# The last expert item of a mixture-of-experts loop handled apart: other items' rows added early, its own output by halves through a one-hot product

## What is computed

```python
def moe_swiglu(h, router, w1, w3, w2):
    logits = (xt @ router).astype(jnp.float32)
    top_val, top_idx = lax.top_k(logits, TOP_K)          # 2 of 8
    gates = jax.nn.softmax(top_val, axis=-1)
    combine = jnp.sum(jax.nn.one_hot(top_idx, N_EXPERTS) * gates[..., None], axis=1)
    out = jnp.zeros((B * T, D), jnp.float32)
    for e in range(N_EXPERTS):
        out = out + combine[:, e:e + 1] * swiglu(xt, w1[e], w3[e], w2[e])
    return out
...
h = h + moe_swiglu(u, m_router[c], m_w1[c], m_w3[c], m_w2[c])
return rmsnorm(h, norm_final)
```

## Time and profile before

| | us |
|---|---|
| median of 3 runs | 1728.95 (1728.02 to 1730.25) |
| the profiled execution's own time | 1729.75 |
| its span | 1727.9 |
| PE busy in the span | 1619.8 (94%) |
| DVE busy | 1234.2 (71%) |
| ACT busy | 966.2 (56%) |
| POOL busy | 43.6 (3%) |

### The profile page before, as it was taken

How to read it: one execution, slowest core, us unless ns; L and a number is a source line. 1 busy time by engine, 2 the same in 40 slices (tenths; PEclk the granted TensorE clock), 3 DMA queues, 4 the chain that set the end, 5 groups by cost and what they waited for, 6 DMA issues and landing times.

```text
span 1727.9 us, 25936 instructions
## 1 busy us (share of the span) xinstructions
PE 1619.8 (94%) x10286; PEld 1360.6 (79%) x10286; DVE 1234.2 (71%) x928; ACT 966.2 (56%) x780; POOL 43.6 (3%) x25
## 2 busy tenths in 40 slices
PE   4999889899979997889999999999999999999993
PEld 3777875899869886778888888888888888888883
DVE  4575345555447444489888898898898898988985
ACT  2321222444333344367777777777777777777773
POOL 1000500000000000010000000000000000000000
PEclk9999999999989998989999999999999999999997
DMA  4447213555544452379999999999999999999972
GB/s 165 146 146 264 81 52 126 192 176 191 193 163 170 164 193 70 133 300 421 375 369 406 357 389 388 358 404 387 346 412 364 374 391 366 395 387 352 411 305 85
DMA packets 70893, 473.76 MB, mean 274 GB/s; under 512 B 7728, under 2 KB 7856, under 8 KB 17840
## 3 DMA queue, kind: packets, MB, share of 16 engines
q1 hardware_dynamic: 66512, 456.69, 69.0%
q10 hardware_dynamic: 3168, 11.96, 1.8%
q0 software_dynamic: 1152, 4.19, 0.7%
HBM read 452.37 MB, written 20.45 MB: 274 GB/s over the span
## 4 chain that ended last, share of the span: by engine, by line
issue 56%; PE 37%; DVE 4%; ACT 1%; DMA 1%; POOL 0%; DVEq 0%; POOLq 0%; ACTq 0%
PE ps L1218 36%; DVE mem L965 0%; PE ps L1230 0%; ACT workr L577 0%; DVE mem L859 0%; DMA work<-back,itab 0%; DMA h<-x 0%; ACT work L561 0%; DVE work L1051 0%; PE ps L1566 0%; DVE work L815 0%; POOL sent L537 0%; DVE mem L951 0%; DVE h L843 0%; DVE pairs_r L835 0%
## 5 line engine op out<-in xcount | busy, mean ns | idle before, releaser
L1218 PE MATMUL ps<-pairs_r,workr 128*128 128x512 f32 x2856 | 659.5, 389 | 1.8 <-DVE workr L1057 1.8
L1218 PEld LDWEIGHTS ps<-pairs_r,workr 128*128 128x128 f32 x2856 | 535.3, 188 | 112.7 <-DVE workr L1057 2.0
L1218 PE MATMUL ps<-workr 128*128 128x512 f32 x2016 | 481.2, 392 | 2.5 <-DVE workr L1156 2.5
L1218 PEld LDWEIGHTS ps<-workr 128*128 128x128 f32 x2016 | 374.2, 188 | 78.9 <-issue 2.7
L1168 DVE TENSOR_TENSOR workr<-ring,workr 128x2048 fp32r<-128x2048 f32 x168 | 383.3, 2290 | 58.3 <-ACT workr L746 58.3
L1168 DVE TENSOR_TENSOR pairs_r<-ring,pairs_r 128x2048 fp32r<-128x2048 f32 x168 | 382.0, 2290 | 22.5 <-ACT pairs_r L746 20.0
L746 ACT ACTIVATE pairs_r<-ring 128x2048 fp32r<-128x2048 f32 x168 | 322.6, 1920 | 112.6 <-PE ps L1218 110.4
L746 ACT ACTIVATE workr<-ring 128x2048 fp32r<-128x2048 f32 x168 | 321.2, 1917 | 43.8 <-PE ps L1218 39.2
L1218 PE MATMUL ps<-mem 64*64 64x64 f32 (+8 forms) x3384 | 251.3, 267 | 28.5 <-DVE mem L859 11.1
L1218 PEld LDWEIGHTS ps<-mem 64*64 64x64 f32 (+5 forms) x3384 | 193.8, 154 | 84.9 <-issue 60.0
L835 DVE TENSOR_TENSOR pairs_r<-ring,pairs_r 128x2048 fp32r<-128x2048 f32 x68 | 156.0, 2294 | 145.7 <-ACT pairs_r L585 144.5
(11 more groups left out here) (195 smaller groups left out, 574.9 us busy)
## 6 DMA issues: line engine op xcount, KB each, us to landing
ring<-mstream SPq DMA_DIRECT2D x336, 1024.0 KB, 6.9
ring<-pstream SPq DMA_DIRECT2D x65, 1024.0 KB, 4.9
mem<-rstream SPq DMA_DIRECT2D x10, 2048.0 KB, 8.2
sent<-work SPq DMA_DIRECT2D x1, 6144.0 KB, 19.3
back<-work SPq DMA_DIRECT2D x1, 6144.0 KB, 35.5
back<-work ACTq DMA_DIRECT2D x9, 512.0 KB, 8.8
work<-sent ACTq DMA_DIRECT2D x8, 512.0 KB, 7.8
h<-x SPq DMA_DIRECT2D x1, 1024.0 KB, 6.3
```

What stands on the lines that cost most here:

```text
L1218: ins = nc.tensor.matmul(*args, **kw)
```

## The change

- The loops of PE, ACT and DVE run one item less; the last item is written out behind them by the same function with `last` set. In it ACT no longer fetches tokens for a next item, the four dummy units and the gather are gone, and SP's dummy fetches with them.
- POOL gathers rows from `back` during the last item, as soon as the output of the item before it has landed there. What the last item owes is still zero in `back`. DVE adds the four tiles at steps j = 2 to 5 of the last item.
- Which rows of the last item belong to which token is put into two one-hot matrices `hot` on DVE ahead of the loop; PE transposes them at the start of the last item, and DVE stores them as `hotT`.
- The last w2 product (`output_by_halves`) finishes bank 4 and then bank 5. Each half is split in a high and a low part (ACT, DVE), and PE multiplies `hotT` by them, which puts the last item's output rows at their tokens: eight matmuls in all. DVE adds the four results times the gate (`share`, L1265 of the new file) to `h`.
- The final norm sums squares of four half tiles, multiplies tile 0 by the gain before the root is there, and writes the output in two DMAs.

The core of the diff (helpers, new semaphores and buffer addresses left out):

```diff
 # SP
-            for n in range(AHEAD):
-                i = PRE + NE * E_UNITS + n
-                sp.wait_ge(s_lo, extras * E_UNITS + (i - RING + 1))
-                sp.dma_start(unit(i)[:, 0:64], mstream[n, :, 0:64]).then_inc(s_w[i % RING], 16)
-            sp.wait_ge(s_fin, TT)
-            sp.dma_start(out, xn_).then_inc(s_out, 16)
+            for t in range(TT):
+                sp.wait_ge(s_fin, t + 1)
+                sp.dma_start(out[:, t, :], xn_[:, t, :]).then_inc(s_out, 16)
 # POOL
-            pool.wait_ge(s_yall, 1)
-            for t in range(TT):
-                for n in range(2):
-                    nc.gpsimd.indirect_dma_start(
-                        yg[:, t, n, :], None, back, bass.IndirectOffsetOnAxis(itab[:, 8 + 2 * t + n:9 + 2 * t + n], 0)
-                    ).then_inc(s_yl[2 * t + n], 16)
+            pool.wait_ge(s_sent, 64)
+            pool.wait_ge(s_yw, extras * 16 + 16 * (NE + 1))
+            pool.wait_ge(s_hotp, 1)
+            link(nc.gpsimd.tensor_tensor(rw(332, 4), rw(50, 4), ones[:, 0:4], ALU.mult))
+            for i in range(2 * TT):
+                nc.gpsimd.indirect_dma_start(
+                    fetched[i], None, back, bass.IndirectOffsetOnAxis(itab[:, 8 + i:9 + i], 0)
+                ).then_inc(s_yl[i], 16)
 # ACT, behind the loop
-            store_output(extras + NE)
-            a.wait_ge(s_yw, extras * 16 + 16 * (NE + 2))
-            act_f(small[:, 190:191], ones[:, 0:1], ACT.Sqrt).then_inc(s_yall, 1)
+            with a.Fori(0, extras + (NE - 1)) as e:
+                item(e, False)
+            item(extras + (NE - 1), True)
+            a.preload_act_table(ACT.Sqrt)
+            for c in range(2):
+                a.wait_ge(s_lo6, c + 1)
+                act_f(yh[:, c * 512:(c + 1) * 512], ps[:, 4 + c, :], ACT.Copy).then_inc(s_yh, 1)
+            for i, (c, t, _) in enumerate(spread):
+                a.wait_ge(s_hf, 2 * TT + i + 1)
...
+                act_f(junk[:, 0:512], hv[:, t, c * 512:(c + 1) * 512], ACT.Square, scale=1.0 / 32.0,
+                      accum_out=ss[:, 8 + 2 * c + t:9 + 2 * c + t]).then_inc(s_ss, 1)
 # DVE, ahead of the loop: loc, inl, share and the one-hot matrices, 11 instructions; in the last item
+                    if last and j == 0:
+                        v.wait_ge(s_hotp, 1)
+                        V.tensor_copy(hotT, ps[:, 2, 0:256]).then_inc(s_hotT, 1)
...
+                    if last and 2 <= j < 2 + 2 * TT:
+                        add_fetched(j - 2)
 # DVE, behind it
+            for c in range(2):
+                cs = slice(c * 512, (c + 1) * 512)
+                v.wait_ge(s_yh, c + 1)
+                V.tensor_tensor(yl[:, cs], ps[:, 4 + c, :], yh[:, cs].bitcast(F32), ALU.subtract).then_inc(s_ylo, 1)
+            for i, (c, t, bank) in enumerate(spread):
+                v.wait_ge(s_last, i + 1)
+                dst = hv[:, t, c * 512:(c + 1) * 512]
+                V.scalar_tensor_tensor(out=dst, in0=ps[:, bank, :], scalar=rw(328 + t, 1), in1=dst, op0=ALU.mult,
+                                       op1=ALU.add).then_inc(s_hf, 1)
...
+            V.tensor_tensor(hg, hv[:, 0, :], gfin, ALU.mult).then_inc(s_hg, 1)
+            V.scalar_tensor_tensor(out=m, in0=ss[:, 8:10], scalar=EPS, in1=ss[:, 10:12], op0=ALU.add,
+                                   op1=ALU.add).then_inc(s_ms, 1)
+            rsqrt(m, r, small[:, 184:186])
+            V.tensor_scalar(xn_[:, 0, :], hg, r[:, 0:1], None, ALU.mult).then_inc(s_fin, 1)
+            V.scalar_tensor_tensor(out=xn_[:, 1, :], in0=hv[:, 1, :], scalar=r[:, 1:2], in1=gfin, op0=ALU.mult,
+                                   op1=ALU.mult).then_inc(s_fin, 1)
 # PE: output_by_halves
+                    for c in range(2):
+                        for half in range(2):
+                            for g in range(2):
+                                ins = M3(ps[:, 4 + c, :], parts((actTh, actTl), i % 2, 2 * half + g),
+                                         parts(w[half], g, slice(c * 512, (c + 1) * 512)),
+                                         start=False, stop=(half == 1 and g == 1), skip_group_check=True)
+                        ins.then_inc(s_lo6, 1)
 # PE, behind the last item
+            for c in range(2):
+                mine = [x for x in spread if x[0] == c]
+                cs = slice(c * 512, (c + 1) * 512)
+                if c:
+                    pe.wait_ge(s_ylo, 1)
+                pe.wait_ge(s_yh, c + 1)
+                for _, t, bank in mine:
+                    M(ps[:, bank, :], hotT[:, t * P:(t + 1) * P], yh[:, cs], start=True, stop=False)
+                pe.wait_ge(s_ylo, c + 1)
+                for _, t, bank in mine:
+                    M(ps[:, bank, :], hotT[:, t * P:(t + 1) * P], yl[:, cs], start=False, stop=True).then_inc(s_last, 1)
```

More of the change, by code:

```diff
@@ L419, in first_unit @@
             return 6 * j - 2 if j else 0
+        spread = [(0, 0, 0), (0, 1, 1), (1, 0, 2), (1, 1, 3)]
         block = ctx.enter_context(nc.Block())
@@ L738, in _, with item @@
             a.preload_act_table(ACT.Silu)
-            with a.Fori(0, extras + NE) as e:
+            def item(e, last):
                 def split_e(lo, hi):
@@ L759, in _ @@
                     split_e(u, u + 1)
-                    if j == 2:
+                    if j == 2 and not last:
                         a.wait_ge(s_sent, 64)
@@ L1621, in _, with item @@
             extras = pe.value_load(itab[0:1, 0:1], min_val=0, max_val=EXTRA)
-            with pe.Fori(0, extras + NE) as e:
+            def item(e, last):
                 def units(n, dims, **sizes):
```

119 lines of the change are left out of this document (84 added, 35 removed).

## The result

The changed kernel took 1709.42 us, the median of 5 runs (1708.97 to 1718.04), against 1728.95 before (5 runs, 1724.91 to 1730.25). The ratio is 0.9897, with a 95% interval of 0.988 to 0.9914. The profiled execution took 1709.88 with a span of 1708.1.

The account below looks back on a forecast made before the run. PE was taken to bound the items, with a chain without PE behind them. Tail -14.8 and end of the last product -0.6 make -15.4; from the median 1728.95 that gives 1713.5 us, range 1712.0 to 1717.5.

Parts of the forecast that it names:

- The bound and the cover: Items: PE sets the time, so work beside it on DVE, ACT or DMAs is free until their reserve is used.
- E: End of the last w2 product, forecast to move by -0.6 us: gather's transposes save 0.8, one-hot transposes cost 0.2.
- The tail: Chain behind the last w2 product to the span's end: 12.0 us against 26.8 before, so 14.8 less.
- The halves of the last product: Last w2 product: first half finishes 2.8 us before the end, so its copy and subtraction are done by then.
- the gain's multiplication: Final norm: DVE multiplies tile 0 by the gain on the path, 1.18 us, with ACT's last Square beside it.
- The reserve of the last item: Last item: 9 us in the pairs, 5.6 in the ring, 3.7 before L1173's delay reaches PE; PE sees nothing.
- the bound of 10: Sign of being wrong: ACT waiting on the ring by more than 10 us in sum.
- The longer tail: Rival behind the last product: slower output DMA, adds and hops, up to +2.5 us, 1716.0; 0.08 including part of a stall.
- The crowded item: Rival in the last item: fetches, late refills and adds stall PE by 4 to 9 us, 1718 to 1722; chance 0.05.
- The item's code: Rival at the written-out last item: code fetched block by block, 35 us in all, 1748; chance 0.03.
- How the numbers follow: Chances: 0.81 for 1712.0 to 1716.0, 0.02 for shorter than 1712; range given 1712.0 to 1717.5.
- The first part: Start of the run to the first product of the first item: forecast change 0.

Follow-up runs that it names:

- both_halves: Changed kernel with banks 4 and 5 of the last w2 product finished together, in the order of before; 1714.18 us, ratio 0.9918.
- gain_with_scale: Changed kernel with tile 0 multiplied by the gain while being scaled, not ahead of the root; 1714.63 us, ratio 0.9918.
- after_again: The changed kernel run a second time, no edit; 1713.01 us, ratio 0.9908.
- after_third: The changed kernel run a third time, no edit; 1714.65 us, ratio 0.9916.
- fetch_behind: Changed kernel with POOL's fetches held until the last item's copies and the four adds put behind the subtraction; 1723.85 us, ratio 0.9971.
- peel_only: Kernel before with only the last item written out behind the loops of PE, DVE and ACT; 1728.77 us, ratio 0.9999.
- fetch_three_times: Changed kernel with every tile fetched three times (6 MB, not 2) and adds at j = 3 to 6; 1723.49 us, ratio 0.9974.
- adds_four_times: Changed kernel with three more unused multiply-adds on DVE per fetched tile; 1725.15 us, ratio 0.9979.

## Why the prediction was right in its sum and wrong in its number

1. **The bound and the cover.** Right. PE is busy for 119.00 of 119 us of the last item in the trace after with all that the change put beside it, and E moved by 0.7 (-0.6 forecast).
2. **The tail.** Right, step by step. Counted from E, 0.1 before ACT's pickup at 1696.29, the trace after has the adds from +1.3 (+1.4 forecast), their end at +4.1 (+4.2), the root at +5.3 (+5.4) and its end at +6.7 (+6.8), tile 1 scaled at +8.7 (+8.8), and the span's end at +11.9 (+12.0). The two profiled executions have 975.28 - 959.61 = 15.67 us between them in items and tail, with the mean of the three profiles of the old items and tail (975.02) it is 15.4, the forecast sum.
3. **Why the tail fell so far.** Partly misread. The halves of the last product were to take a copy and a subtraction off the path; both_halves shows that the old order had that cover nearly whole. And the gain's multiplication stands on the path only as long as ACT's squares do: the two end together.
4. **The reserve of the last item.** Right that no PE wait is seen in the trace after, wrong on what protects it. I worked it out from the pairs (9 us) and the ring (5.6 us) and gave L1173, now L1214, 3.7 us against its own delay alone. But the split of a unit that PE needs only later stands ahead of L1214 in DVE's order, so a late unit in the ring delays L1214 too, and the smallest reserve, 3.7 us, counts for both. In the trace after little of it is left at the step where gain_with_scale halted:

```profile
1614.80 8.32 PE L1290 MATMUL ps<-pairs_r,workr 128*128 128x512 f32 x36
...
1615.85 0.68 DVE L1214 TENSOR_TENSOR workr<-ps,workr 128x512 fp32r<-128x512 f32 x1
```

L1214 ends at 1616.5 and PE takes its result up behind the first 12 of the 36 matmuls, at about 1617.5: 1.0 us. ACT's four ring waits ahead of it are 5.8 us in sum here and 7.1 in gain_with_scale (1.35, 1.84, 3.34, 0.58), 1.3 more, and that was enough for a halt of 0.3. Over all items ACT waits for the ring by 10.3 us in the trace after, which passes the bound of 10 that the prediction set as a sign of being wrong, with no PE wait; in after_again it is 4.7 and in after_third 2.3, and in fetch_behind, without fetches in the item, 0.2. So that sum is no good sign: it varies from one execution to the next, and the place of the late units decides.

The two rows of ring waits of the trace after, 752 to 1700 us, against 0.6 in the earlier trace rows:

```profile
ACT pairs_r L764 <- DMA ring<-mstream: 8.3, 7, 1.8
...
ACT workr L764 <- DMA ring<-mstream: 2.0, 4, 0.6
```

5. **The rivals.** The longer tail did not come (11.9 against up to 14.5). The crowded item is real: it cost 0.6 to 0.7 us in two profiles at the planned load, far below the 4 to 9 that its rival was priced at, and 8.2 and 12.2 with more load. The item's code is refuted by peel_only.
6. **The step that failed: "How the numbers follow", and the base that the sum was made against.** I subtracted 15.4 from a median of three runs, and gave my range 1.5 us below that result, for the terms of the sum alone. The first part's change was put at nothing, with no spread. The base was not as fixed as that: the first part measured -4.20 between the two profiles, the same instructions up to the first product take anywhere from 747.6 to 756.3 us, and the executions of one program spread over 9 to 10 us. Three runs from 1728.02 to 1730.25 did not show it. The profile of before gave the hint that I did not follow, in windows of its three parts (columns as in the earlier trace rows):

```profile
0.00:738.00 738.00, 663.44 (x5924) 567.62 (x5924) 373.07 (x399) 246.48 (x286) 34.76 (x17) 0.96 0.43 154
738.00:752.00 14.00, 7.89 (x42) 7.61 (x42) 10.85 (x51) 4.93 (x6) 3.86 (x3) 0.63 0.54 220
752.00:1701.00 949.00, 948.34 (x4320) 785.39 (x4320) 840.33 (x466) 709.70 (x481) 1.12 (x2) 1.00 0.95 373
```

   PE is idle for 80.7 of the first 752 us and 0.7 of the next 949, and the granted clock is below 1.00 only in the first two. What can vary stands there. The forecast value was near the mean of the changed kernel's 17 executions (1712.8 against 1713.5); the measured median of five was at the lower end of their spread, by chance: three of those five executions are at or below 1709.42, and one of the twelve others. That the forecast value lies so near the mean agrees with the sum; the number missed through the base and this low draw. Eight of the 17 lie below my lower bound of 1712.0 and one above the upper. With the spread of the base in it, the range had to be about 1709 to 1718, an estimate from these 17 executions.

What stays open is why the clock is granted later in one execution than in the next, and whether it is the cause or goes with one.

## What to carry to other kernels

Before a saving is subtracted from a time, cut the profile where the change begins, and ask how far the part ahead of it repeats; a range needs that spread even where every term of the sum is sure. The tail behind the last product is a plain chain, and a sum of row durations with a hop of 0.1 for each hand-over came within 0.2 us over 12. A reserve is to be worked out for the last in an engine's order: what is late ahead of it delays it too, so the smallest reserve in the queue is the one that counts. One profile without a halt does not show that a reserve holds; two in eight had one here.

## What the runs showed of the hardware

- Beside the stream of weights (1 MB for each 2.8 us of PE), indirect fetches of 512 KB slow each unit: in fetch_three_times ACT takes one every 3.76 us while fetches are in flight (1604.66, 1608.45, 1612.19, 1615.99). That is 1.5 MB in 3.76 us, about 417 GB/s, if one fetch goes with each unit; the 10 us windows of fetch_three_times from 1605 to 1635 us give 416 to 421 GB/s, and the 20 us windows of the trace after from 1600 to 1660 us 415 to 422.
- POOL's issue of an indirect DMA took 0.95 to 0.97 us in fetch_behind, with little beside it, and 0.97, 2.73, 1.89 and 1.90 in the last item. The fetches landed after 11.6 us (median) in the trace after and after 5.6 in fetch_behind, where no stream ran beside them.
- A written-out copy of a 120 us loop body cost nothing on PE (peel_only: busy for 120.00 of 120 us, ratio 0.9999), its code loaded during the run.
- A halt of PE of 0.3 to 0.4 us inside a row of 36 matmuls cost 0.6 to 0.7. Behind a halt of 2.7 us in adds_four_times the granted clock was 0.76 for the next 24 matmuls, behind one of 5.5 in fetch_three_times 0.74; behind three further halts of 1.1 to 2.7 us in adds_four_times the products took their usual time.
- The first 750 us, the same instructions with PE in gaps, spread by 8.7 us over 13 profiles, nearly all of it in the busy time of the same 5966 matmuls (666.8 to 676.6 us), while the 960 us behind them, with PE full, repeated to 0.01 us in three profiles of the changed kernel.
